# Norm vectors of the K, V, query and gate weights: from POOL's multiplications into the split operations of ACT and DVE

## What is computed

```python
def rms_norm(x, g):
    xf = x.astype(jnp.float32)
    y = xf * lax.rsqrt(jnp.mean(xf * xf, axis=-1, keepdims=True) + EPS)
    return (y * g.astype(jnp.float32)).astype(x.dtype)
...
u = rms_norm(x, g_pre[1]);  s = rms_norm(x, kv_norm)
k_new, v_new = s @ w_k, s @ w_v
q, gate      = u @ b_w_in           # halves of the output columns
z = q @ k.T / sqrt(128) + bias;  log_keep = where(mask, log_sigmoid(-z), 0)
suffix = reversed exclusive cumsum of log_keep over keys
attn = where(mask, exp(log_sigmoid(z) + suffix), 0);  o = attn @ v
out = (o * silu(gate)) @ b_w_out
```

## Time and profile before

| | us |
|---|---|
| median of 3 runs (lowest, highest) | 2024.17 (2018.96, 2031.26) |
| the profiled execution | 2034.04 |
| its span | 2032.4 |
| PE busy in it | 1847.5 (91%) |
| DVE busy | 1126.7 (55%) |
| ACT busy | 785.6 (39%) |
| POOL busy | 272.0 (13%) |

### The profile page before, as it was taken

The page is one execution under the profiler, slowest core; times in us unless marked ns, Lnnn a source line. Parts: engine busy times, 40 slices in busy tenths (PEclk is TensorE's granted clock), DMA queues, the critical chain, the costliest instruction groups (busy, mean ns, idle before and its releaser), DMA issues.

```text
span 2032.4 us, 35373 instructions
## 1 busy us (share of the span) xinstructions
PE 1847.5 (91%) x13466; PEld 1761.1 (87%) x13466; DVE 1126.7 (55%) x1844; ACT 785.6 (39%) x1132; POOL 272.0 (13%) x184
## 2 busy tenths in 40 slices
PE   4999999999997999947999999999997799899995
PEld 3899999999997999937989989999996676689993
DVE  4766666666666222296667577577576433442226
ACT  3244444444434222232555455465455222232222
POOL 4100000000000001133322322322321000001110
PEclk9999999999998999957999999999998677799995
DMA  5323232322322323342222222222224346412324
GB/s 194 95 88 89 84 92 83 90 85 84 92 67 59 92 83 92 106 151 83 76 61 63 85 63 69 79 73 63 84 63 133 106 146 181 148 53 85 91 84 154
DMA packets 278697, 191.50 MB, mean 94 GB/s; under 512 B 7899, under 2 KB 250715, under 8 KB 277979
## 3 DMA queue, kind: packets, MB, share of 16 engines
q1 hardware_dynamic: 277708, 188.03, 31.1%
q0 software_dynamic: 896, 2.23, 0.4%
HBM read 174.26 MB, written 15.97 MB: 94 GB/s over the span
## 4 chain that ended last, share of the span: by engine, by line
PE 74%; DVE 12%; issue 7%; ACT 6%; DMA 1%; POOL 0%; SPq 0%; ACTq 0%; DVEq 0%; POOLq 0%
PE PS L591 20%; PE PS L593 20%; PE PS L592 20%; PE Z L876 4%; PE PS L847 2%; PE PS L858 1%; PE Z L591 1%; PE Z L593 1%; PE Z L592 1%; DVE Y L1463 1%; ACT WS L937 1%; ACT L1122 1%; DVE WS L1241 1%; DMA prow<-in_state_h_dram 1%; DVE T L1503 1%
## 5 line engine op out<-in xcount | busy, mean ns | idle before, releaser
L591 PE MATMUL PS<-U,WS 128*128 128x272 f32 x3712 | 1089.3, 293 | 60.3 <-DVE U L1470 34.1
L593 PE MATMUL PS<-U,WS 128*128 128x272 f32 x3712 | 1085.2, 292 | 0.0
L592 PE MATMUL PS<-U,WS 128*128 128x272 f32 x3712 | 1081.7, 291 | 0.0
L591 PEld LDWEIGHTS PS<-U,WS 128*128 128x128 f32 x3712 | 712.0, 192 | 67.6 <-issue 35.5
L592 PEld LDWEIGHTS PS<-U,WS 128*128 128x128 f32 x3712 | 712.1, 192 | 0.8
L593 PEld LDWEIGHTS PS<-U,WS 128*128 128x128 f32 x3712 | 711.5, 192 | 0.0
L1241 DVE TENSOR_TENSOR WS<-raw,WS 128x1024 fp32r<-128x1024 f32 (+1 forms) x240 | 305.9, 1275 | 500.5 <-ACT WS L937 498.0
L937 ACT ACTIVATE WS<-raw 128x1024 fp32r<-128x1024 f32 (+1 forms) x240 | 246.7, 1028 | 601.8 <-PE PS L593 596.1
L506 POOL TENSOR_TENSOR raw<-raw,GN 128x1024 f32<-128x1024 f32 x80 | 159.6, 1996 | 436.2 <-DMA raw<-in_b_w_in_dram 340.6
L518 POOL TENSOR_TENSOR T<-T 128x544 f32<-128x544 f32 x60 | 88.4, 1473 | 379.4 <-ACT T L1033 376.9
L515 POOL COPY T<-T 128x544 f32<-128x544 f32 x4 | 3.2, 790 | 852.2 <-ACT T L1033 825.4
(11 more groups left out here) (212 smaller groups left out, 2025.9 us busy)
## 6 DMA issues: line engine op xcount, KB each, us to landing
raw<-in_a_w_in_dram SPq DMA_DIRECT2D x80, 512.0 KB, 3.8
raw<-in_b_w_in_dram SPq DMA_DIRECT2D x64, 512.0 KB, 4.1
raw<-in_a_w_out_dram SPq DMA_DIRECT2D x32, 512.0 KB, 3.8
raw<-in_b_w_out_dram SPq DMA_DIRECT2D x32, 512.0 KB, 3.8
KPG<-in_cache_k_dram SPq DMA_DIRECT2D x64, 256.0 KB, 2.9
VPG<-in_cache_v_dram SPq DMA_DIRECT2D x64, 256.0 KB, 2.9
T<-scratch_x SPq DMA_DIRECT2D x32, 272.0 KB, 2.9
scratch_x<-T SPq DMA_DIRECT2D x16, 272.0 KB, 2.1
```

The costliest lines, as they stand in the source:

```text
L591: pe.matmul(psum, w_hi, x_hi, start=first, stop=False)
L592: pe.matmul(psum, w_hi, x_lo, start=False, stop=False)
L593: return pe.matmul(psum, w_lo, x_hi, start=False, stop=last)
```

## The change

POOL no longer multiplies. In stage D ACT's high part is made by 8 instructions of 128x128, one per K tile, each a copy with the norm vector's column of that K tile as its per-partition scale. DVE's low part is made by 8 instructions of 128x128, each `raw * gain - high`. Only the last of the 8 signals. Both wait once, ahead of the first. ACT waits for the load in place of `w_fold`. POOL's program in stage D is only the storing of K and V. In stage E and the other stages `high` and `low` stay as they are. The last round of `pair_b` on DVE is taken out of its loop, and the low part of unit E0 stays a plain one.

```diff
-            def fold(of, m, slot, gain):
-
-                pool.wait_ge(unit_in[slot], of * 8 + 16 * (m // 2 + 1))
-                g = GN[:, slot * UT:(slot + 1) * UT, gain:gain + 1].to_broadcast([P, UT, P])
-                pool.tensor_tensor(raw[:, slot], raw[:, slot], g, ALU.mult).then_inc(w_fold, 1)
...
-            folds(0, True)
-            with pool.Fori(1, NKV) as k:
-                folds(k, False)
+            with pool.Fori(0, NKV) as k:
+                pool.wait_ge(kv_t_out, k * 2 + 2)
+                store_kv(k, 0)
+                store_kv(k, 1)
...
+            def high_gain(k, n):
+
+                slot, gain = n % 2, G_KV if n % 20 < 4 else G_PRE1
+                act.wait_ge(unit_done, k * 20 + (D0 + n - 1))
+                act.wait_ge(unit_in[slot], k * 160 + 16 * ((D0 + n) // 2 + 1))
+                for c in range(UT):
+                    ins = nc.scalar.activation(WS[:, slot, 0, c, :], raw[:, slot, c, :], ACT.Copy,
+                                               scale=GN[:, slot * UT + c, gain:gain + 1])
+                ins.then_inc(w_high, 1)
...
-                            high(k * 20 + (D0 + off + s + 1), (s + 1) % 2, 0, folded=True)
+                            high_gain(k, off + s + 1)
...
+            def low_gain(k, n):
+
+                slot, gain = n % 2, G_KV if n % 20 < 4 else G_PRE1
+                dve.wait_ge(w_high, k * 20 + (D0 + n + 1))
+                for c in range(UT):
+                    ins = V.scalar_tensor_tensor(WS[:, slot, 1, c, :], raw[:, slot, c, :], GN[:, slot * UT + c, gain:gain + 1],
+                                                 WS[:, slot, 0, c, :].bitcast(F32), ALU.mult, ALU.subtract)
+                ins.then_inc(w_low, 1)
...
-                        low(k * 20 + (D0 + off + s + 1), (s + 1) % 2)
+                        if last and s == 3:
+                            low(E0, 0)
+                        else:
+                            low_gain(k, off + s + 1)
```

More of the change, by code:

```diff
@@ L176, in build @@
         x1_kept = sem("x1_kept")
-        w_fold = sem("w_fold")
         k_high = sem("k_high")
@@ L531, in _ @@
                 add_square(2 * KD - 2 + n, n, 1, False)
-                fold(0, D0 + n, n, G_KV)
             for o in range(KD):
@@ L928, in _, with high @@
         def _(act):
-            def high(m, slot, n, tiles=UT, before=True, folded=False):
+            def high(m, slot, n, tiles=UT, before=True):
                 if before:
                     act.wait_ge(unit_done, m - 1)
[L933 to L936, removed]
+                act.wait_ge(unit_in[slot], n * 16 + 16)
                 nc.scalar.activation(WS[:, slot, 0, 0:tiles, :], raw[:, slot, 0:tiles, :], ACT.Copy).then_inc(w_high, 1)
+            def high_gain(k, n):
[6 more added lines that the diff above has]
+                ins.then_inc(w_high, 1)
             def root(k):
@@ L1038, in pair_b @@
                     if not (first and n == 0):
-                        high(i * 6 + (B0 + n + 1), (n + 1) % 2, i * 3 + (B0 + n + 1) // 2, B_TILES[(n + 1) % 3],
-                             folded=last and n == 5)
+                        if last and n == 5:
+                            high_gain(0, 0)
+                        else:
+                            high(i * 6 + (B0 + n + 1), (n + 1) % 2, i * 3 + (B0 + n + 1) // 2, B_TILES[(n + 1) % 3])
                     if n == 4:
@@ L1051, in _ @@
             root(1)
-            high(D0 + 1, 1, (D0 + 1) // 2, folded=True)
+            high_gain(0, 1)
             for o in range(KD):
@@ L1056, in _ @@
                 square(2 * KD + o, o % 2, Y[:, o, :])
-            high(D0 + 2, 0, 0, folded=True)
+            high_gain(0, 2)
             root(2)
@@ L1441, in out_tile, with pair_b @@
                 V.tensor_copy(halves(y_one(Y[:, bass.ds(of + n, 1), :])), PS[:, par, :, 0:HALF]).then_inc(strip_out, 1)
-            def pair_b(i, first):
+            def pair_b(i, first, last=False):
                 for n in range(6):
-                    if not (first and n == 0):
+                    if last and n == 5:
+                        low_gain(0, 0)
+                    elif not (first and n == 0):
                         low(i * 6 + (B0 + n + 1), (n + 1) % 2, B_TILES[(n + 1) % 3])
@@ L1451, in _ @@
             pair_b(0, True)
-            with dve.Fori(1, KD // 2) as i:
+            with dve.Fori(1, KD // 2 - 1) as i:
                 pair_b(i, False)
+            pair_b(KD // 2 - 1, False, True)
             for n in range(5):
@@ L1458, in _ @@
             norm(1)
-            low(D0 + 1, 1)
+            low_gain(0, 1)
             def residual(o, gain, done):
@@ L1476, in _ @@
             x1_rest(KD - 1)
-            low(D0 + 2, 0)
+            low_gain(0, 2)
             norm(2)
@@ L1532, in head_out, with pair @@
                 V.tensor_tensor(y, y, o_sum, ALU.mult).then_inc(o_out, 1)
-            def pair(k, off, g=None, att=None, tail=None, gate=None, turn=False, units=True, first=False):
+            def pair(k, off, g=None, att=None, tail=None, gate=None, turn=False, units=True, first=False, last=False):
                 for s in range(4):
@@ L1597, in group @@
                 pair(k, 12, g=2, att=(k, 1), tail=(k, 0), gate=(k, 1))
-                pair(k, 16, g=3, att=(k, 2), tail=(k, 1), gate=(k, 2))
+                pair(k, 16, g=3, att=(k, 2), tail=(k, 1), gate=(k, 2), last=not whole)
                 if whole:
```

## The result

| | runs | median us | lowest to highest |
|---|---|---|---|
| before | 4 | 2027.72 | 2018.96 to 2035.21 |
| changed | 4 | 2110.03 | 2106.92 to 2114.51 |

The ratio is 1.0409 (95% interval 1.0359 to 1.0460): slower. The profiled execution of the changed kernel took 2106.92 us, against 2034.04 before: +72.9, where the medians differ by 82.3.

The account below looks back on a forecast made before the run. It took PE's work (30.9 us a head) and the loop ACT and DVE hand back and forth as nearly equal bounds. Stage D's +81 us, other terms 0, on the 2024.2 median gave 2105 us, range 2068 to 2145.

Parts of the forecast that it names:

- The high part: ACT's eight scaled copies of a unit in stage D: 2.49 us less 1.06, +1.43 us a unit.
- The low part: DVE's eight multiply-and-subtract pieces of a unit in stage D: 2.24 us less 1.23, +1.0 us a unit.
- What lies on the path: Head in stage D: ACT's extra counts in four steps, DVE's in steps 1 to 3; 29.38 us becomes 38.1.
- The stage: Stage D: 15 heads of 38.1 us, less 2.4, give 569.1 against 488.5, +81 us.
- Turn pairs: Between groups of heads in stage D: ACT's waits for PE cover the 2.43 us more; 0, at most 7.
- Around the residual: Low parts ahead of the residual on DVE cost +2.5 us; PE's wait behind it ends some 2 earlier; together 0.
- PE's idle time: Heads in stage D: PE idle some 7 us a head, behind sp_rest and at_rest.
- POOL and the queues: POOL loses 80 instructions, 159.6 us, all beside other work; loads get more room, stores come no later; 0.
- POOL's stalls were the price: Rival, stage D: a unit gains under 0.4 us, stalls go, PE bounds; 25 us less, 1999; 4 in 100.
- Cheap pieces: Rival: pieces cost somewhat over the lower bounds, +35 to +50 us, 2059 to 2074; 10 in 100.
- no difference: Rival: extra of 0.8 us a unit leaves a head at 32.6 us, as now; 2024; 4 in 100.
- PE's clock: Rival, heads: waiting PE drops to its lower clock and becomes the bound; 125 us on top, 2230; 6 in 100.

Follow-up runs that it names:

- without a gain: Changed kernel with the norm vector left out: one ACT and one DVE instruction per unit, no POOL multiplication; 2005.01 us, 0.9868 of before.
- whole in step 0: Changed kernel with DVE's low part as one instruction without the norm vector in step 0 of each attention head; 2114.40 us.
- POOL busy: Changed kernel in which POOL multiplies attention tiles that nothing uses in stage D, once a unit; 2103.24 us.
- A signal per piece: Changed kernel with a signal for each of ACT's pieces and DVE waiting piece by piece; 2040.29 us, 1.0053 of before.

## Why the prediction was right

It gave 2105 us (2068 to 2145), slower with 0.92. The median is 2110.03. The mechanism held, as the experiments show. That the number is off by only 5 us is in part luck: by the profiled executions +81 was forecast and +72.9 measured, with 4 us too many for the heads, 2 too few for the turn pairs and nothing for the samples' stage, which came out 6 us shorter. Point by point, by its own steps:

- *The high part.* Forecast 0.39 us long and 0.30 apart, 2.49 a unit. Measured 0.387, and 2.44 for eight, so (2.44 - 0.39)/7 = 0.293 apart, +1.38 against +1.43. The fixed part taken from rows of 544 columns held at 128.
- *The low part.* Forecast 0.35 long and 0.27 apart, 2.24 a unit. Measured 0.347, and 2.19 for eight: 0.263 apart, +0.96 against +1.0. The Trainium skill's 60 ns (Perfetto Trace Analysis, optimizing Scalar/DVE operations) gave +0.35 as an estimate. With a per-partition scalar the trace differs from it: 0.263 less 128 x 1.04 ns leaves 0.13 us of fixed part. With constants in place of that scalar the same operation starts 0.34 us apart at 256 columns in this trace (L1504, 1203.62 and 1203.96), which leaves 0.07. So the page's figure holds for the plain form, and about half of the 0.13 goes with the scalar.
- *What lies on the path.* Forecast steps of 10.01 + 1.43 = 11.4, then 9.1, 9.9 and 7.7. Measured 11.40, 9.08, 9.92, 7.57. That they meet to 0.1 us has two small errors in it: the two parts cost 2.34 and not 2.43, and the bare steps 1 and 2, read in the last group, are 0.08 shorter there than in the loop's groups (6.65 against 6.73 without a gain). The three-against-four count of the low part was tested by itself (whole in step 0) and held.
- *The stage.* Forecast +81, measured +76.2. The term that was mis-sized is "15 x 38.1", less 2.4: 569.1 against 564.7, 4.4 us too much. In the middle of a group heads take 37.97 us. But the first head of each group takes 37.50, 37.50, 37.52 and 37.28, since its step 0 lasts 10.9 and not 11.4, and that is 2.6 of the 4.4.
- *Turn pairs.* Forecast 0, measured +2.1, of which 1.7 in the third, whose time before was 26.91. It was not the cover that failed. PE stood still for 2.07 us just before that pair, against 1.24 before the second, and its matmuls then start 0.23 us apart until 1493.6, so the pair's first step takes 8.77 us at a granted clock of 0.81, in place of 7.25 at 1.00:

```profile
1489.18 0.44 PE L732 MATMUL Z<-U,KVP 128*128 128x384 f32 x1 [2.07 <-DVE U L1528]
...
1489.83:1498.60 8.77, 8.56 (x53) 8.18 (x53) 5.24 (x14) 4.97 (x12) 0.00 (x0) 0.81 0.28 80
```
- *Around the residual.* Forecast +2.5 ahead, -2 behind, 0 together. Measured: the residual starts at 879.78 against 876.36, +3.4, of which about 1 us was there already at D0's high part, so +2.4. PE's wait behind it ends at 944.12 against 943.04, +1.1, so -2.3 behind. The prediction read the earlier trace rows wrongly in one point: the stalled norm operation at 937.39 does not stand beside the two multiplications that end at 931.37, but beside POOL's next one:

```profile
937.23 1.92 POOL L506 TENSOR_TENSOR raw<-raw,GN 128x1024 f32<-128x1024 f32 x1 [5.87 <-DMA raw<-in_b_w_in_dram]
```

That one is gone as well, and the operation is back to its width:

```profile
939.12 0.72 DVE L1298 TENSOR_TENSOR T<-RS 128x544 f32<-128x544 f32 x1
```

PE's wait, which ended at 943.04 before:

```profile
944.12 0.51 PE L572 MATMUL PS<-U,WS 128*128 128x272 f32 x1 [3.52 <-DVE WS L1287]
```

From there to the first sigmoid (982.42 against 979.70) another 1.6 us were lost. Of these 1.4 are the longer high part that stands just ahead of that sigmoid (2.45 us at 978.65, against 1.06 at 977.33 before).
- *PE's idle time.* Forecast 7 us a head, measured 37.97 - 33.05 = 4.9. PE's own work took 2.1 us longer than in the earlier trace rows, at a granted clock of 0.96 against 1.00; in the next head it is 0.91, with 34.27 us busy. The waits by the table for stage D (980 to 1626; total us, count, longest):

```profile
PE Z L732 <- DVE U L1528: 39.6, 27, 2.4
...
PE Z L732 <- DVE Y L1534: 23.7, 11, 2.2
...
PE Z L710 <- DVE U L1512: 12.4, 19, 4.0
```

Most of it is at the `pv` passes (L732), which wait for at_rest (L1528) and for the finished output of the head before (L1534), and the smaller part at the `later` passes (L710), behind sp_rest (L1512). The part on what is late next had named sp_rest alone.

- *POOL and the queues.* Forecast 0. No load is late for ACT: in the table of waits for stage D, ACT's high part (L923) waits for PE alone, 30.9 us in ten waits,

```profile
ACT WS L923 <- PE PS L574: 30.9, 10, 4.1
```

against 57.8 us in 33 waits before.

*The rivals.* "POOL's stalls were the price" was right in its mechanism: the stalls were real, in a head 1.7 us, and a kernel without them and without pieces is 23 us faster. It failed in its condition, that the pieces cost under 0.4 us a unit; they cost 2.34. "Cheap pieces" and "no difference" fell with the piece times. "PE's clock" fell as a bound of the heads: in stage D it is 0.96, and ACT waits for PE nowhere in a head. The falls are real all the same; they took 1.5 us in the third turn pair, and 1.0 us of the step of the kernel before that is shown above (7.71 against 6.73).

## What to carry to other kernels

Before work is moved off an engine that is mostly idle onto two others, lay out the loop in which these hand work back and forth, and add the price in every step in which nothing else covers it. Cutting an instruction into pieces costs a fixed part each time (here 0.09 us on ACT and as much again for the scale, 0.13 on DVE with its scalar), and here the cost came back, and not all of it, only where the follower was signalled by the piece. A vector along the contracted dimension can be applied to either factor of a product: put it on the one that is touched fewer times. And where an engine's work stalls a neighbour, look up in the trace when it runs and what it meets there.

## What was not expected of the hardware

The stage behind stage D, attention for the samples, has a granted clock that differs from execution to execution, and its length with it. Its windows, from the first to the last of its 512 matmuls with the cached keys, before, in the changed kernel, and with POOL busy:

```profile
1594.40:1768.80 174.40, 160.22 (x898) 123.42 (x896) 63.37 (x95) 39.02 (x66) 0.00 (x0) 0.75 0.50 151
```

```profile
1673.20:1841.20 168.00, 153.80 (x897) 119.42 (x896) 63.46 (x95) 39.11 (x66) 0.00 (x0) 0.78 0.53 156
```

```profile
1684.50:1837.20 152.70, 138.49 (x898) 105.44 (x896) 63.71 (x95) 39.12 (x66) 0.00 (x0) 0.87 0.58 172
```

With the same matmuls it takes 174.4, 168.0 and 152.7 us at a clock of 0.75, 0.78 and 0.87. In all three PE is idle for 14.2 us, so the difference is all in how long PE's matmuls took; over the ten profiled executions the length runs from 152.7 to 180.4 (clock 0.73). No edit touches its code. It moves the total by more than some effects studied here, so single runs are compared by their stage, not by their total: with POOL busy the total was 3.7 us less although stage D was 9.9 us more, since this stage was 15.3 us shorter. Why the clock differs there was not tried.

A signal per piece is 11.0 us slower than before by the profiled executions and 12 by the medians. In the profiled ones 1.8 of it lie ahead of the first sigmoid, 5.5 in the stage, and 3.7 behind it, where the attention for the samples took 180.4 us.
